# Group A's attention: queries and keys normed and turned by thirds, the next pair's products spread over all units

## The reference

```python
h = rmsnorm(x); z = h @ w_in          # columns split into qa, ka, va (group A), qb, kb, vb, ob, gates
qa = partial_rope(rmsnorm(qa, q_norm), pos)    # per head of 64
ka = partial_rope(rmsnorm(ka, k_norm), pos)
o_a = combine_by_denominators([dilated_band_stats(qa, ka, va, w, d) for (w, d) in DILATED_PATTERNS])
h_b = mlstm_prompt(qb, kb, vb, ig, lf)         # group B
x += concat(rmsnorm_A(o_a), sigmoid(ob) * rmsnorm_B(h_b)) @ w_out
x += ConvGLU(rmsnorm(x)); x += gate(rmsnorm(x)) * (p @ w_ple_proj)
```

## Time and profile before

| | us |
|---|---|
| median of 3 runs | 3724.94 |
| lowest, highest | 3723.93, 3727.58 |
| the profiled execution | 3723.14 |
| its span (first to last instruction) | 3721.3 |
| PE busy | 3452.1 (93%) |
| DVE busy | 2163.5 (58%) |
| ACT busy | 872.2 (23%) |

### The profile page before, as it was taken

One profiled execution on the slowest core, in us unless ns is written; L12 is line 12 of the kernel. 1 busy time (PEld: TensorE's weight loads), 2 busy tenths in 40 slices (PEclk: granted clock), 3 DMA queues, 4 the chain that ended last, 5 costly groups with the idle time before them and its releaser, 6 DMA issues. The chain is left out here.

```text
span 3721.3 us, 49482 instructions
## 1 busy us (share of the span) xinstructions
PE 3452.1 (93%) x19817; PEld 3128.8 (84%) x19817; DVE 2163.5 (58%) x4724; ACT 872.2 (23%) x1608; POOL 596.1 (16%) x497
## 2 busy tenths in 40 slices
PE   4999999978899999999988999998799999999989
PEld 4777767767899999998977777676699999999988
DVE  5565546656755555557565553566666555555573
ACT  3222232212311111113232222222122111111131
POOL 2000011210221221221110011111103122222211
PEclk7999889967999999999989999898599999999999
DMA  4111112353111111110211110133411111111101
GB/s 137 35 35 41 41 37 63 74 152 78 46 57 46 46 46 46 46 47 28 82 53 30 41 41 18 51 88 80 148 48 57 46 50 53 35 58 46 38 29 62
DMA packets 208141, 209.69 MB, mean 56 GB/s; under 512 B 34468, under 2 KB 180836, under 8 KB 205808
## 3 DMA queue, kind: packets, MB, share of 16 engines
q1 hardware_dynamic: 207912, 206.53, 18.8%
HBM read 175.03 MB, written 31.64 MB: 56 GB/s over the span
## 5 line engine op out<-in xcount | busy, mean ns | idle before, releaser
L706 POOL TENSOR_TENSOR wlo<-raw,whi 128x512 fp32r<-128x512 f32 (+3 forms) x488 | 595.4, 1256 | 3066.8 <-ACT whi L1174 3066.8
L721 PE MATMUL ps<-hi,wlo 128*128 128x344 f32 x2880 | 931.9, 324 | 25.0 <-DVE wb L1965 15.5
L722 PE MATMUL ps<-lo,whi 128*128 128x344 f32 x2880 | 925.0, 321 | 0.0
L723 PE MATMUL ps<-hi,whi 128*128 128x344 f32 x2880 | 924.6, 321 | 0.0
L721 PEld LDWEIGHTS ps<-hi,wlo 128*128 128x128 f32 x2880 | 546.1, 190 | 28.2 <-DVE wb L1965 16.1
L722 PEld LDWEIGHTS ps<-lo,whi 128*128 128x128 f32 x2880 | 545.8, 189 | 0.6
L723 PEld LDWEIGHTS ps<-hi,whi 128*128 128x128 f32 x2880 | 545.9, 190 | 0.0
L721 PE MATMUL ps<-whi,lo 128*128 128x512 f32 (+5 forms) x1152 | 452.8, 393 | 34.4 <-POOL wlo L706 25.6
L723 PE MATMUL ps<-whi,hi 128*128 128x512 f32 (+5 forms) x1152 | 435.1, 378 | 0.0
L722 PE MATMUL ps<-wlo,hi 128*128 128x512 f32 (+5 forms) x1152 | 435.0, 378 | 0.0
L1977 DVE TENSOR_TENSOR X<-X,ps 128x344 f32<-128x344 f32 x528 | 268.5, 512 | 196.9 <-PE ps L723 196.3
(11 more groups left out here) (268 smaller groups left out, 4336.1 us busy)
## 6 DMA issues: line engine op xcount, KB each, us to landing
raw<-in_w_up SPq DMA_DIRECT2D x44, 1024.0 KB, 5.1
raw<-in_w_in SPq DMA_DIRECT2D x112, 256.0 KB, 4.4
raw<-in_w_down SPq DMA_DIRECT2D x22, 1024.0 KB, 4.9
kvb<-in_cache_win_k SPq DMA_DIRECT2D x48, 256.0 KB, 3.5
cache<-in_cache_win_v SPq DMA_DIRECT2D x36, 256.0 KB, 5.7
x_scratch<-X SPq DMA_DIRECT2D x8, 1032.0 KB, 6.8
X<-x_scratch SPq DMA_DIRECT2D x4, 2064.0 KB, 14.3
raw<-in_w_out SPq DMA_DIRECT2D x8, 1024.0 KB, 6.7
```

The costliest lines, as they stand in the source:

```text
L706: pool.tensor_tensor(out=wlo[:, s, r], in0=raw[:, s, r], in1=whi[:, s, r].bitcast(F32), op=ALU.subtract).then_inc(w_split, 1)
L721: nc.tensor.matmul(out, a_lo, b_hi, start=first, stop=False)
L722: nc.tensor.matmul(out, a_hi, b_lo, start=False, stop=False)
L723: return nc.tensor.matmul(out, a_hi, b_hi, start=False, stop=last)
```

## The change

- **Thirds.** Queries and keys are normed, rotated and turned by thirds of three tiles (0 to 2, 3 to 5, 6 to 8; the third one includes the sample tile, on all 128 partitions, whose unused rows are set to 0 once). Turned thirds go through one PSUM bank (5): three transposes of queries, ACT's copy, three of keys into the same bank, DVE's copy.
- **Second place.** Pairs 0 and 2 keep turned queries and keys in `zt`'s columns OG:ZW (which only group B's pairs fill), pairs 1 and 3 in `qT` and `kT` as before. So a pair can be turned while the one before is in its units, and `scores(p + 1, 0)` stands in unit 15 of pair p, `values(p, 15)` in unit 0 of pair p + 1.
- **Where the norm stands.** Pair p + 1's first third in units 5 to 7 (turned in 8), its second in 11 to 13 (turned in 14), its last in units 0 to 2 of its own units (turned in 3). Pair 0: the first third before its units, the second in units 0 and 1 (turned in 1), the last in 2 to 4 (turned in 4).
- **Root.** ACT computes exp(-0.5 ln(s / 64 + eps)) (`head_root`), DVE corrects it with one Newton step of 4 small instructions; before, DVE did 13.
- **Products.** `FILL` gives the number of pair p + 1's products in each of the 16 units; none are done ahead of the units.
- **Outputs by head.** Squares, sums and stores of outputs go by head (64 columns).

```diff
-def ahead(p, u):
-    return min(NPROD, (20 if p == 0 else 4) + 7 * u)
+FILL = (6, 6, 6, 2, 6, 5, 5, 5, 1, 1, 5, 5, 6, 6, 3, 4)
+def ahead(u):
+    return sum(FILL[:u])
...
+        qkA = [[zt[:, z, 0:NT, OG:ZW] for z in (1, 0)],
+               [t.rearrange("p (t n) -> p t n", n=P) for t in (qT, kT[:, :])]]
...
 PE
+                def turn_third(p, x, j):
+                    n = 3 * p + x
+                    if j:
+                        pe.wait_ge(*at(q_evac, n + 1))
+                    else:
+                        pe.wait_ge(*at(qk_norm, n + 1))
+                        pe.wait_ge(*at(k_evac, n))
+                    for i, t in enumerate(range(NT)[third(x)]):
+                        mm = nc.tensor.transpose(ps[:, 5, i * P:(i + 1) * P], zt[:, p % 2, t, j * P:(j + 1) * P], ident[:, :])
+                    mm.then_inc(turned, 1)
...
-                products(1, 0, 16)
                 pe.wait_ge(*at(rcol_done, 3))
-                turn_qk(0)
+                for j in range(2):
+                    turn_third(0, 0, j)
+                scores(0, 0)
+                pe.wait_ge(*at(z_done, NT + 1))
                 for p in range(PAIRS):
-                    products(p + 1, 16 if p == 0 else 0, ahead(p, 0))
-                    scores(p, 0)
                     for u in range(NU):
-                        products(p + 1, ahead(p, u), ahead(p, u + 1))
+                        products(p + 1, ahead(u), ahead(u + 1))
                         if u + 1 < NU:
                             scores(p, u + 1)
+                        elif p + 1 < PAIRS:
+                            scores(p + 1, 0)
+                        if p and u == 3:
+                            turn_third(p, 2, 0)
+                        elif p + 1 < PAIRS and u in (8, 14):
+                            turn_third(p + 1, u // 14, 0)
                         turn_p(p, u)
                         if u:
                             values(p, u - 1)
-                    if p + 1 < PAIRS:
-                        turn_qk(p + 1)
-                    values(p, NU - 1)
+                        elif p:
+                            values(p - 1, NU - 1)
+                        if p == 0 and u in (1, 4):
+                            for j in range(2):
+                                turn_third(0, (u + 2) // 3, j)
+                        elif p and u == 3:
+                            turn_third(p, 2, 1)
+                        elif p + 1 < PAIRS and u in (8, 14):
+                            turn_third(p + 1, u // 14, 1)
+                values(PAIRS - 1, NU - 1)
...
 ACT
+                def head_root(p, x):
+                    hc = slice(12 * x, 12 * x + 12)
+                    act.wait_ge(*at(qk_ssq, 3 * p + x + 1))
+                    do(nc.scalar.activation(qs36[:, 1, hc], qs36[:, 0, hc], ACT.Ln, scale=1.0 / HD, bias=eps[:, :]))
+                    do(nc.scalar.activation(qs36[:, 1, hc], qs36[:, 1, hc], ACT.Exp, scale=-0.5), qk_rs, wait=False)
...
 DVE
-                        if p + 1 < PAIRS:
-                            if u in (5, 10):
-                                norm_squares(p + 1, u // 10)
-                            elif u in (6, 11):
-                                norm_root(u // 10)
-                            elif u in (7, 12):
-                                norm_scale(p + 1, u // 10)
-                            elif u in (8, 13):
-                                norm_rope(p + 1, u // 10)
+                        if p == 0:
+                            if u == 0:
+                                norm_squares(0, 1)
+                                norm_scale(0, 1)
+                            elif u == 1:
+                                norm_rope(0, 1)
+                                evac_third(0, 1)
...
+                        if p + 1 < PAIRS:
+                            if u in (5, 11):
+                                norm_squares(p + 1, u // 11)
+                            elif u in (6, 12):
+                                norm_scale(p + 1, u // 12)
+                            elif u in (7, 13):
+                                norm_rope(p + 1, u // 13)
+                            elif u in (9, 15):
+                                evac_third(p + 1, u // 15)
+                        if u == 10:
+                            head_squares(p, 0)
```

More of the change, by code:

```diff
@@ L143, in far, with third, turned_value @@
     return sum(1 for x in range(u) if UNITS[x % NU][1] >= 4)
-def ahead(p, u):
-    return min(NPROD, (20 if p == 0 else 4) + 7 * u)
+FILL = (6, 6, 6, 2, 6, 5, 5, 5, 1, 1, 5, 5, 6, 6, 3, 4)
+def ahead(u):
+    return sum(FILL[:u])
+def third(x):
+    return slice(3 * x, min(3 * x + 3, NT))
+def turned_value(p, half):
+    return 3 * p + half + 1 if p < PAIRS else 3 * PAIRS + 2 * (p - PAIRS) + half + 1
 def ahead_b(c):
@@ L1231, in round_pair, with evac_third @@
                     round_block(B + 2 * p + 1)
+                def evac_third(p, x):
+                    act.wait_ge(*at(turned, 2 * (3 * p + x) + 1))
+                    q3 = qkA[p % 2][0][:, third(x), :]
+                    src = ps[:, 5, 0:q3.shape[1] * P].rearrange("p (t n) -> p t n", n=P)
+                    do(nc.scalar.activation(q3, src, ACT.Copy), q_evac, wait=False)
                 def evac_q(p):
                     for half in range(2):
-                        act.wait_ge(*at(turned, 4 * p + 2 * half + 1))
+                        act.wait_ge(*at(turned, 2 * turned_value(p, half) - 1))
                         do(nc.scalar.activation(qT[:, half * 512:(half + 1) * 512], ps[:, (5, 1)[half], :], ACT.Copy), q_evac, wait=False)
@@ L1264, in _ @@
                     z_evac(0, t)
-                act.wait_ge(*at(gz_abs, 1))
-                do(nc.scalar.activation(gt[:, :, :], gt[:, :, :], ACT.Exp, scale=-1.0))
-                do(nc.scalar.activation(gt[:, :, :], gt[:, :, :], ACT.Ln, bias=one1[:, :]), gz_ln)
-                evac_q(0)
+                    if t == 5:
+                        head_root(0, 0)
+                evac_third(0, 0)
+                probabilities(0, 0)
                 for p in range(PAIRS):
-                    for t in tiles(0, ahead(p, 0)):
-                        z_evac(p + 1, t)
-                    probabilities(p, 0)
                     for u in range(NU):
-                        for t in tiles(ahead(p, u), ahead(p, u + 1)):
+                        for t in tiles(ahead(u), ahead(u + 1)):
                             z_evac(p + 1, t)
@@ L1515, in norm_rope, with norm_squares @@
[L1515 to L1525 removed]
+                def norm_squares(p, x):
+                    w = slice(3 * x, 3 * x + 3)
+                    dve.wait_ge(*at(z_done, (NT + 1) * p + 3 * x + 3))
+                    zz = zt[:, p % 2, w, 0:256]
+                    sqv = rowr[:, 0:768].rearrange("p (t c) -> p t c", t=3)
+                    do(v.tensor_tensor(out=sqv, in0=zz, in1=zz, op=ALU.mult))
+                    do(v.tensor_reduce(out=s36[:, w, :], in_=sqv.rearrange("p t (h d) -> p t h d", h=4), axis=AX.X, op=ALU.add), qk_ssq, wait=False)
@@ L1640, in sample_max @@
+                outputs(PAIRS - 1, NU - 1)
+                head_squares(PAIRS - 1, 1)
                 def sample_max():
```

244 lines of the change are left out of this document (140 added, 104 removed).

## The result

| | before | after |
|---|---|---|
| median, us | 3724.94 (3723.93 to 3728.9 in 7 runs) | 3739.68 (3722.87 to 3752.59 in 7 runs) |
| profiled execution, us | 3723.14 | 3752.59 |
| its span, us | 3721.3 | 3750.8 |
| layer 0's last `values` start at, us | 517.2 | 537.8 |

The ratio is 1.0038 with a 95% interval of 1.0024 to 1.0052: slower, where 3689 was forecast. The seven runs after lie much wider apart than those of before, a hint that something in the kernel now happens in some executions and not in others. The profiled one is the slowest of the seven: what is read from its trace is the upper end of what the change costs.

What follows compares the result with a forecast made beforehand. PE bounds it, losing 48.6 of 396.9 us a layer, mostly where the norm stands beside bare units. Work 353.8 plus waits 26.4 makes 380.2, gain 16.7; with 1.2, 17.9 a layer, twice 35.8: 3724.9 - 36 = 3689 us, range 3658 to 3714.

Steps and rivals of the forecast that it cites:

- unit 8: 0.55 + 1.70 = 2.3, waits 0.75: Turning in unit 8: PE has 2.3 us of products and scores, the third is ready at 3.05, so PE waits 0.75.
- rope 2.3: DVE's rope of one third, sized from half-size rows: 0.95 + 3/4 of 0.88 + two small ones 0.6 = 2.3 us.
- Short waits bring the low clock: Rival: each of nine short-wait places adds 1.8 us of low clock, 16 a layer, giving 3722 us; chance 0.12.
- the turning places run a unit late: Rival: 11 turning places each wait a rope, a copy and a half-clock spell, 5.75 us each, giving 3770 us; chance 0.06.
- if the turnings of units 8 and 14 wait over 2 us, if the low clock returns in pairs 1 and 2: Two of the signs the prediction named, in the profile after, that would show it wrong.
- Work and cover: Per layer: PE's work sums to 353.8 us, no unit is bound by DVE, and nearly all 48.6 us lost can go.
- Unit 14: Turning of the second third: PE has 2.1 us of work, waits 0.95, and 0.1 for the queries' copy.
- Unit 3: Turning of the last third, pairs 1 to 3: waits 0.65, then 0.7 more for ACT's copy before the keys.
- Pair 0, unit 1: Turning of pair 0's second third: waits about 4.5, queries' copy 0.9, half clock 1.8; sum 7.2 us.
- Unit 4: Pair 0's last third, turned right behind values: waits the whole 3.05, plus 0.9 and 1.8; 5.8 us.
- Start: First third turned and copied twice with nothing between: 3.0 us, of which 0.7 is work, so 2.3 of waits.
- The rule weighed: Waits under 1 us are priced at their length, against the skill's section on clock swings from brief, frequent idling.

Runs made afterwards that it cites:

- e1: Changed kernel with ACT's rounding, and POOL's split with it, moved from unit 6 to unit 9: 3683.12 us, ratio 0.9881.
- e5: Changed kernel with rounding in unit 9, plus two elementwise DVE steps on scratch ahead of unit 7's rope: 3725.46 us, ratio 0.9996.
- e2: Changed kernel with the next pair's first third turned in unit 9 instead of 8, POOL left in place: 3694.31 us, ratio 0.9910.
- e3: Changed kernel with 5 and 5 products in units 8 and 9 instead of 1 and 1, fewer in some others: 3694.14 us, ratio 0.9906.
- e6: Changed kernel with six products in unit 9 instead of one, one less each in units 7 and 10 to 13: 3722.05 us, ratio 0.9989.

## Why the prediction was wrong

**The step that failed** is "unit 8: 0.55 + 1.70 = 2.3, waits 0.75", and in it the "rope 2.3". That size came from rows in which POOL was idle (the earlier trace rows show POOL at 0.00 in the tail, where the rope of the earlier trace rows stood). In the kernel before, the first half's rope stood in unit 8, three units behind POOL's split in unit 5. The change puts the first third's rope in unit 7 and the split in unit 6, so the two meet. The part-by-part list never put POOL's span beside DVE's new steps. With POOL away the rope took 2.21 us and the wait was 0.55 us, so the arithmetic of the unit was sound. With it, the rope took 3.98 us in pair 1 and the wait was 2.3 to 4.6.

The trace of before had the sign of it. POOL's split there ran from 268.21 to 275.98, and two equal small steps of the root inside and behind it read:

```profile
268.21 7.77 POOL L706 TENSOR_TENSOR wlo<-raw,whi 128x384 fp32r<-128x384 f32 x8 [81.06 <-ACT whi L1174]
```

DVE's timeline:

```profile
275.07 0.95 DVE L1440 TENSOR_SCALAR qs<-qs 128x16 int32<-128x16 int32 x1
276.05 0.17 DVE L1441 TENSOR_SCALAR qs<-qs 128x16 int32<-128x16 int32 x1
```

0.95 against 0.17 us for the same form, 1 us apart in time. A step of DVE beside POOL can be held for about one of POOL's pieces (7.77 / 8 = 0.97 us). The rope has five steps, three of which met POOL: up to 3 us on a third that PE met after 2.3 us of work. The Trainium skill, "SBUF — State Buffer", section "SBUF: two separate sides", says that DVE and GpSimd have one pair of SBUF ports in common, an exclusive lock held for a whole instruction, and that a DVE operation with two SBUF inputs takes it too, against a GpSimd one that reads SBUF, as the split does. By that each of the four steps L1601, L1606 (two) and L1607 of pair 2 could be held for up to one 1.35 us piece, 5.4 us in all; the trace shows 2.10 + 2.64 + 1.20 = 5.94 against 0.96 + 0.63 + 0.26 = 1.85, 4.1 more, and agrees. The small steps L1439 and L1440 have one input only, so its case of two inputs does not cover them, and the trace shows them held too (0.82 and 0.95 us against 0.17).

**The second failure** is the price of a wait's clock. "Short waits bring the low clock" had 1.8 us a place, from the 6.5 us stretch of the earlier trace rows at the start, where products follow. Behind unit 8's wait come transposes, values, scores and one product a unit, and in the profiled execution the low clock stayed for 17 to 20.5 us: 8.5 to 9.6 us a place instead of 1.8. The tail's own stretches in the earlier trace rows (17 us, PE busy 13.67) showed that length in just such units. The fourth rival, "the turning places run a unit late", had the right kind of end and the right lever (3.7 us a place decides), but was spread over 11 places; here six places (three a layer) cost 11.8 us more each than in e1 (35.4 / 3, in the slowest of the seven executions) or 9.4 by the medians (56.6 / 6), and that was enough. It had 0.06. The prediction's sentence on what would make it wrong, "if the turnings of units 8 and 14 wait over 2 us, if the low clock returns in pairs 1 and 2", named both symptoms.

**What held, by e1.** Work and cover: pairs of 100.6, 87.9, 89.4 and 98.2 us against 101, 89, 89 and 99. Unit 14: 0.84 us against 1.05 with its copy. Unit 3: 0.96 + 0.69 = 1.65 in pairs 1 and 2 and 0.61 + 0.69 = 1.3 in pair 3, against 1.35. Pair 0, unit 1: 4.13 + 0.58 and half of 5.8 busy at low clock, 7.6, against 7.2. Unit 4: 3.06 + 0.48 and half of 3.5, 5.3, against 5.8. Start: 1.38 + 0.77 = 2.2 against 2.3, and 1.8 of half clock that wasn't forecast. Scores on `zt` cost nothing: a 7-block group reads 1.77 us on `zt` (363.59, pair 2 of e1) and 1.77 on `kT` (274.23, pair 1). Squares of one head: from the last outputs' transposes to the gate rows 13.14 us against 14.20 before, 1.06 saved against 1.2, although the wait that answers the earlier trace rows grew from 5.58 to 7.1, because PE arrives there earlier:

```profile
PE ps L951 <- DVE rowr L1836: 14.1, 2, 7.1
```

Had the split stayed clear of the rope, 3689 would have been 3683.

**The rule weighed.** The earlier trace rows held for the single short waits. In e1 none of the three waits of 0.55 us or the three of 0.84 had a low stretch behind it; of the three pairs of waits in unit 3 (0.96 or 0.61, then 0.69) one did, for 3.5 us. By the section of the Trainium skill that the prediction named ("TensorE: Matmul & The Clock Gate", "A second HAM failure mode: psum-queue depth-cycling"), as it was read there, all nine should have cost one; the trace shows one. The changed kernel's own trace is less kind to the forecast: of its six pairs of waits in unit 3 (two layers), four had 3.5 us at 0.50 behind them. So single short waits were harmless, and two within some 2 us sometimes were not.

**Still open.** Why the same wait of 2.5 us is followed by nothing, by 3.5 us or by 17 us at half clock in one execution (e5), why waits of 2.65 us (e2) and 2.79 us (e3) in pair 2 had only 3.5 us behind them, and so why the changed kernel's executions lie 30 us apart. The runs show no long stretch in unit 8 where its wait is under 1 us, and shorter ones where products stand close behind it; not what decides in between. That the seven runs differ by these stretches is inferred from their mean clocks (0.923 to 0.930), not seen in traces of each.

## What to carry to other kernels

When a change moves a step in time, lay every engine's timeline over its new place, also those of engines that neither wait nor are waited for there: POOL was busy 16% of the span, nobody waited for it in these units, and it decided the sign. Take a step's duration from a row in which the same neighbours run, or bound it by the worst row of its form (0.17 and 0.95 us stood a microsecond apart). And price a wait of PE by what follows it: with a group of products close behind (e6), waits of 2.8 to 4.9 us brought stretches that cost 1.7 to 5 us more; ahead of nearly bare attention units, a wait of 2.3 us cost up to 9.6 more, four times its length.

## What the runs showed of the hardware

- Plain fp32 steps of DVE with both inputs in SBUF are held by a `tensor_tensor` of POOL: 128x192 went from 0.31 to 1.05 us each (1.32 beside pieces of 512), 128x96 from 0.26 to 1.20, 128x768 from 0.96 to between 1.26 and 2.10. Small steps with one SBUF input went from 0.17 to 0.82 and 0.95. The mask, which reads PSUM and one SBUF tile, was not held: 1.22 us for 128x1024 beside POOL (281.74, changed kernel) and away from it (271.31, e1). POOL's own eight pieces took 8.55 us beside the rope, 8.18 in e1 and 7.77 in the kernel before.
- The granted clock can stay at 0.50 while PE does not idle at all: 17.0 us busy of 17.0 in units with one product each. Being fully busy was not enough to bring it back. The long stretches ended inside a group of five or six products (changed kernel: unit 10), and those of 7 and 10 us in e6 inside unit 9's; stretches of 3.5 us ended ahead of any group (e5, pair 0; e6, pair 1).
- Waits of 0.55 and 0.84 us never brought it down in e1's units; every one of 2.3 us and more in the units of the changed kernel's profiled execution had a stretch behind it, five of e5's six of 2.5 us had one. The step between a harmless and a costly wait is narrow: 1.8 to 4.1 us of DVE's time three times a layer was worth 57 us of 3740.
